# Strassen's seven products for three 1024-column matrix products of a fused decoder block

## What is computed

```python
h  = rmsnorm(x)
P  = h @ W_in                       # columns: NSA q, k/v, gates; retention q, k, v, swish gate g; merge gates gA, gB
yA = nsa_attention(...)             # 8 heads: compressed, selected and window branches
yB = retention(q, k, v, g)          # silu(g) * groupnorm(chunkwise retention)
x  = x + (sigmoid(gA) * (yA @ W_upA) + sigmoid(gB) * (yB @ W_upB)) @ W_o
x  = x + hier_moe(rmsnorm(x))       # 32 experts (1024 -> 256 -> 1024), top 1 of 4 groups, then top 2 of its 8
return rmsnorm(x)
```

## Time and profile before

| | us |
|---|---|
| median of 3 runs (517.6 to 518.23) | 518.21 |
| the profiled execution, whole | 518.49 |
| its span, first to last instruction | 516.7 |
| TensorE busy in it | 482.2 (93%) |
| weight load busy | 303.2 (59%) |
| VectorE / ScalarE / GpSimd busy | 136.4 / 84.0 / 30.3 |
| moved by DMA, mean rate | 150.30 MB, 291 GB/s |

### The profile page before, as it was taken

How to read it: one execution, slowest core, us unless ns; L and a number is a source line. 1 busy time by engine, 2 the same in 40 slices (tenths; PEclk the granted TensorE clock), 3 DMA queues, 4 the chain that set the end, 5 groups by cost and what they waited for, 6 DMA issues and landing times.

```text
span 516.7 us, 6634 instructions
## 1 busy us (share of the span) xinstructions
PE 482.2 (93%) x2704; PEld 303.2 (59%) x2704; DVE 136.4 (26%) x446; ACT 84.0 (16%) x233; POOL 30.3 (6%) x59
## 2 busy tenths in 40 slices
PE   5999999999999999999999899999999989779683
PEld 2599644564568888888865666363654625235231
DVE  1551038025411025202120453222231311112113
ACT  0000024232341000000000532120210211011012
POOL 0600050200000011000001210000000000000001
PEclk9999999999999999999999989999999998989968
DMA  8998667740430430998049399999999999999972
GB/s 270 421 354 216 231 233 299 302 164 23 164 142 22 162 143 20 360 425 354 0 171 430 132 340 404 417 426 426 415 426 422 414 430 409 431 413 427 420 293 84
DMA packets 20573, 150.30 MB, mean 291 GB/s; under 512 B 2915, under 2 KB 3364, under 8 KB 13884
## 3 DMA queue, kind: packets, MB, share of 16 engines
q1 hardware_dynamic: 19008, 146.83, 70.1%
q0 software_dynamic: 1296, 2.92, 2.8%
q10 hardware_dynamic: 236, 0.08, 0.1%
HBM read 147.20 MB, written 2.62 MB: 290 GB/s over the span
## 4 chain that ended last, share of the span: by engine, by line
PE 74%; DMA 12%; SPq 9%; DVE 2%; issue 1%; ACT 1%; POOLq 0%; POOL 0%; DVEq 0%; ACTq 0%
PE bank L597 66%; DMA ring<-in_moe_gate_up 11%; SPq L397 7%; PE bank L924 3%; PE bank L897 3%; SPq L393 2%; PE bank L621 2%; DMA ring<-in_dense 1%; DVE rt L1284 0%; DVE nsa L1587 0%; POOLq L134 0%; PE bank L934 0%; ACT nsa L1218 0%; ACT hT_and_y L1261 0%; ACT hT_and_y L1257 0%
## 5 line engine op out<-in xcount | busy, mean ns | idle before, releaser
L597 PE MATMUL bank<-hT_and_y,ring 128*128 128x256 f32 x384 | 84.3, 379 | 0.2 <-issue 0.2
L597 PEld LDWEIGHTS bank<-hT_and_y,ring 128*128 128x128 f32 x384 | 72.5, 190 | 10.5 <-DVE hT_and_y L1303 0.8
L597 PE MATMUL bank<-ring,hT_and_y 128*128 128x512 f32 (+2 forms) x224 | 78.2, 506 | 0.0
L597 PE MATMUL bank<-ring,nsa 128*32 128x512 f32 (+2 forms) x376 | 58.7, 641 | 8.5 <-DMA ring<-in_moe_gate_up 8.3
L597 PEld LDWEIGHTS bank<-ring,hT_and_y 128*128 128x128 f32 x224 | 37.9, 190 | 36.6 <-issue 36.5
L1587 DVE COPY nsa<-bank 128x512 f32<-128x512 f32 x32 | 22.1, 692 | 102.3 <-PE bank L597 81.4
L597 PEld LDWEIGHTS bank<-cst,nsa 128*128 128x128 f32 x256 | 31.4, 196 | 24.3 <-issue 18.9
L1218 ACT ACTIVATE nsa<-bank 128x512 f32<-128x512 f32 (+1 forms) x40 | 22.2, 555 | 125.8 <-PE bank L597 105.3
L597 PEld LDWEIGHTS bank<-ring,nsa 128*32 128x32 f32 (+1 forms) x376 | 17.2, 123 | 37.2 <-issue 25.8
L597 PE MATMUL bank<-cst,nsa 128*128 128x32 f32 x256 | 34.0, 283 | 1.2 <-DVE nsa L1587 1.2
L924 PE MATMUL bank<-nsa,Tb 128*128 128x128 f32 x256 | 31.4, 282 | 1.0 <-issue 0.7
(11 more groups left out here) (204 smaller groups left out, 482.3 us busy)
## 6 DMA issues: line engine op xcount, KB each, us to landing
ring<-in_moe_gate_up SPq DMA_DIRECT2D x21, 2048.0 KB, 21.5
ring<-in_dense SPq DMA_DIRECT2D x17, 2048.0 KB, 10.2
hT_and_y<-in_moe_gate_up SPq DMA_DIRECT2D x6, 2048.0 KB, 21.1
vr_and_gr<-in_moe_gate_up SPq DMA_DIRECT2D x5, 2048.0 KB, 22.3
windows<-in_moe_down SPq DMA_DIRECT2D x8, 512.0 KB, 17.7
qkT<-in_moe_down SPq DMA_DIRECT2D x8, 512.0 KB, 18.7
nsa<-in_moe_down SPq DMA_DIRECT2D x8, 512.0 KB, 18.5
keys<-in_moe_down SPq DMA_DIRECT2D x8, 512.0 KB, 17.4
```

The lines of the kernel that those rows point to most:

```text
L597: return nc.tensor.matmul(o, l, r, start=s, stop=e)
```

## The change

Each of the three products C = A B is cut into halves of both matrices: A's token tiles and slab halves (a11, a12, a21, a22), B's slab halves and column halves (b11 ...). Seven products of a quarter size (4 matmuls of 128x128 by 128x512 each) replace eight. `hT` gives four left sums, made once by VectorE in the memory of `x` (which is loaded again later); `gate` gives four more in `xs`. Each group's four weight sums are made by VectorE in place in the ring, 128 x 2048 a sum, each after the last reader of what it overwrites. The products go to banks X (first and second product, accumulated), V (third), Z (fifth by its sum), W (sixth, seventh and last, one on top of the other, each read out by VectorE before the next is added). Names: P1, P6, P7 are semaphores of the first, sixth and seventh product; T1 to T4 of the weight sums.

```diff
-BLOCKS = ["qr", "kv0", "kv1", "q", "kr", "w1k", "vr0", "w1v", "vr1", "gr0", "gr1",
+BLOCKS = ["qr", "kv0", "kv1", "q", "kr", "w1k", "w1v", "vr0", "vr1", "gr0", "gr1",
...
+        + ["S0.4", "S0.5", "S1.4", "S1.5", "grX", "grV", "S0.6", "S0.7", "S1.6", "S1.7", "grZ", "PcT", "PV0", "PV1", "grW"]
+        + ["PT4.0", "PT4.1", "PT5.0", "PT5.1", "rTq0", "rTq1", "PV2", "rTk0", "rTk1"]
...
# SyncE
-            first_dw(4)
             sp.wait_ge(*is_full("PV3"))
             first_dw(7)
             load(BLOCKS.index("out0"))
+            for t in range(TT):
+                sp.dma_start(x[:, t, :], a["x"][0, t * P:(t + 1) * P, :]).then_inc(s_x[t], 16)
...
-            sp.wait_ge(s_out0_used, 1)
+            sp.wait_ge(*is_full("outW"))
             first_gu(4)
+            first_dw(4)
# TensorE
+            def product(o, l, r, first=True, last=True, ks=range(4)):
+                for k in ks:
+                    ins = nc.tensor.matmul(o, l[:, k, :], r[:, k, :], start=first and k == 0, stop=last and k == 3, skip_group_check=True)
+                return ins
...
+            product(oX[:, :], a11, b11, True, False).then_inc(s_P1, 1)
+            oV = begin("grV")
+            done("grV", product(oV[:, :], h_sums[:, 3], b22))
+            pe.wait_ge(s_P1_kept, NTH["gr"])
+            done("grX", product(oX[:, :], a12, b21, False, True))
+            scores(0, 3)
+            scores(1, 3)
+            oZ = begin("grZ")
+            pe.wait_ge(s_T1, NTH["gr"])
+            done("grZ", product(oZ[:, :], h_sums[:, 0], b11))
             pe.wait_ge(s_pc, 1)
             transposes("PcT", ...)
-            scores(0, 3)
-            scores(1, 3)
             have("vs", "vwg", "PcT")
             attend(0)
             attend(1)
+            oW = begin("grW")
+            pe.wait_ge(s_T2, NTH["gr"])
+            product(oW[:, :], h_sums[:, 1], b22, True, False).then_inc(s_P6, 1)
+            prob_transposes(4)
+            prob_transposes(5)
+            pe.wait_ge(s_T3, NTH["gr"])
+            pe.wait_ge(s_P6_read, NTH["gr"])
+            product(oW[:, :], h_sums[:, 2], b12, False, False).then_inc(s_P7, 1)
+            turn_rotated(0, 0)
+            turn_rotated(0, 1)
+            pe.wait_ge(s_T4, NTH["gr"])
+            pe.wait_ge(s_P7_read, NTH["gr"])
+            done("grW", product(oW[:, :], a22, b21, False, True))
...
             for i in range(KT):
+                if i == 5:
+                    oX = begin("outX")
+                    pe.wait_ge(s_mrg, 4)
+                    product(oX[:, :], a11, b11, True, False).then_inc(s_P1, 1)
                 o = begin(f"up{i}")
# ScalarE
             swish(0, 0)
-            swish(1, 0)
-            o = take("PcT")
-            copy("PcT", PcT[:, :], o[:, 0:S])
             exps(6)
             exps(7)
+            o = take("PcT")
+            copy("PcT", PcT[:, :], o[:, 0:S])
# VectorE
+            def first_weight_sum(group):
+                b11, b12, _, _ = quarters(group)
+                dve.wait_ge(s_P1, NTH[group])
+                V.tensor_tensor(b11, b12, b11, ALU.subtract).then_inc(s_T1, 1)
+            def third_weight_sum(group):
+                V.tensor_tensor(b12, b22, b12, ALU.subtract).then_inc(s_T3, 1)
+            def second_weight_sum(group):
+                dve.wait_ge(*is_full(f"{group}V"))
+                V.tensor_tensor(b22, b22, b11, ALU.subtract).then_inc(s_T2, 1)
+            def fourth_weight_sum(group):
+                V.tensor_tensor(b21, b21, b22, ALU.subtract).then_inc(s_T4, 1)
...
             biased(5)
+            first_weight_sum("gr")
...
             scaled(5)
+            third_weight_sum("gr")
+            second_weight_sum("gr")
+            fifth_product("gr")
-            swish(0, 0)
-            swish(1, 0)
             biased(6)
             biased(7)
+            swish(0, 0)
+            sixth_product("gr")
+            fourth_weight_sum("gr")
             scaled(6)
             scaled(7)
+            seventh_product("gr")
```

More of the change, by code:

```diff
@@ L315, in cols, with quarters, left, results @@
             return slot(block)[:, 0:KT * n].rearrange("p (k n) -> p k n", k=KT)
+        def quarters(group):
+            if group == "out":
+                w = [slot(f"out{i}").rearrange("p (k n) -> p k n", k=4) for i in range(2)]
+                return w[0][:, :, 0:512], w[0][:, :, 512:1024], w[1][:, :, 0:512], w[1][:, :, 512:1024]
+            w = [cols(f"{group}{i}", 512) for i in range(2)]
+            return w[0][:, 0:4, :], w[1][:, 0:4, :], w[0][:, 4:8, :], w[1][:, 4:8, :]
+        def left(v):
+            return v[:, 0:4, 0:P], v[:, 4:8, 0:P], v[:, 0:4, P:S], v[:, 4:8, P:S]
+        def results(group):
+            v = vr if group == "vr" else y
+            return v[:, 0, 0:512], v[:, 0, 512:D], v[:, 1, 0:512], v[:, 1, 512:D]
+        def piece_ready(piece):
+            n = NTH["out"]
+            return dict(out0=is_emptied("outX"), out1=(s_P6_read, n), out2=(s_P7_read, n), out3=is_emptied("out3"),
+                        out4=is_emptied("out4"))[piece]
         def dense(block):
@@ L741, in _ @@
             done("cmpkv", ins)
[L742 to L745, removed]
+            pe.wait_ge(s_T4, NTH["vr"])
+            pe.wait_ge(s_P7_read, NTH["vr"])
+            done("vrW", product(oW[:, :], a22, b21, False, True))
             have("cmpkv")
@@ L811, in _ @@
             wn = slot("upn").rearrange("p (k n) -> p k n", k=4)
+            a11, a12, a21, a22 = left(gate[:, 0, :, :])
+            b11, b12, b21, b22 = quarters("out")
             for i in range(KT):
+                if i == 5:
+                    oX = begin("outX")
+                    for b in ("out0", "out1"):
+                        pe.wait_ge(*loaded(b))
+                    pe.wait_ge(s_mrg, 4)
+                    product(oX[:, :], a11, b11, True, False).then_inc(s_P1, 1)
                 o = begin(f"up{i}")
@@ L1106, in _ @@
             nc.scalar.activation(hid2[:, :], hid2[:, :], ACT.Tanh, scale=0.7978845608028654).then_inc(s_th, 1)
-            for t in range(TT):
-                o = take(f"vr1{t}")
-                copy(f"vr1{t}", vr[:, t, 512:1024], o[:, :])
+            probs_out(2)
+            probs_out(3)
             o = take("cmpkv")
@@ L1210, in _ @@
             normed(1)
-            seed(3)
+            seed(2)
             exps_router(1)
@@ new lines, in fifth_product, with sixth_product @@
+            def fifth_product(group):
+                _, c12, c21, c22 = results(group)
+                dve.wait_ge(s_P1_kept, NTH[group])
+                o = take(f"{group}Z")
+                freed(f"{group}Z", V.tensor_tensor(c22, o[:, :], c21, ALU.add))
+                o = take(f"{group}V")
+                dve.wait_ge(*is_emptied(f"{group}Z"))
+                freed(f"{group}V", V.tensor_tensor(c12, o[:, :], c22, ALU.add))
+            def sixth_product(group):
+                c12 = results(group)[1]
+                dve.wait_ge(s_P6, NTH[group])
+                dve.wait_ge(*is_emptied(f"{group}V"))
+                V.tensor_tensor(c12, ps(f"{group}W")[:, :], c12, ALU.add).then_inc(s_P6_read, 1)
@@ new lines, in seventh_product, with last_product @@
+            def seventh_product(group):
+                c22 = results(group)[3]
+                dve.wait_ge(s_P7, NTH[group])
+                V.tensor_tensor(c22, ps(f"{group}W")[:, :], c22, ALU.add).then_inc(s_P7_read, 1)
+            def last_product(group):
+                c21 = results(group)[2]
+                o = take(f"{group}W")
+                freed(f"{group}W", V.tensor_tensor(c21, o[:, :], c21, ALU.add))
+            for i in range(1, 4):
+                dve.wait_ge(s_h, i)
+            dve.wait_ge(*is_emptied("R"))
```

321 lines of the change are left out of this document (218 added, 103 removed), and 6 rows, old and new, of the table JOBS.

## The result

| | kernel before | changed kernel |
|---|---|---|
| median of four runs each, same session | 518.22 us (517.6 to 518.5) | **523.69 us** (522.78 to 524.52) |
| ratio to the kernel before | | 1.0115 (95%: 1.0088 to 1.0141) |
| profiled execution: span | 516.7 us | 521.3 us |
| its own time | 518.49 us | 523.5 us |
| mean granted clock of TensorE | 0.976 | 0.960 |

The change is slower by 1.15%, 5.5 us. I had forecast 517.3 with a range to 520.8, so the time lies outside of it, on the side of rival 1, though not by its mechanism.

What follows compares the result with a forecast made beforehand. The end was taken as set by a pauseless transfer stream, started when the first batch's GU0 is done. Terms from -10.5 us (products) summed to -1.2, 0.3 given back: 517.6 profiled, 517.3 us as median; range 514.5 to 520.8.

Steps and rivals of the forecast that it cites:

- rival 1: In-place weight sums on VectorE are slower than the rows say; at 3.0 us a sum 520.9 us; chance 0.18.
- the sums of 2.3 us: Each VectorE weight sum, two operands of 2048 columns, takes 2.3 us; bounds 1.5 and 2.45 us.
- the pause in front of `attend(0)`: In the gate, TensorE waits for ScalarE's copy of PcT, queued behind two exps: 7.5 us.
- the reader of P7: In the gate, TensorE's last product waits for VectorE's reading of the seventh product: 0.7 us.
- the bank of outX: Output product: outX shares a bank with up4, so P1 waits until VectorE has read up4 twice: 0.85 us.
- The fall of the clock: Behind the pause at the first attend, TensorE takes 3.6 us for 1.9 us of work: 1.7 us lost.
- The step that failed first: Transfers up to expert 6's load: through at 306.9, 0.6 us before GU0 is done at 307.5; no cost.
- - 1.7 (order and waits of the end): Output product, routers and first gather up to GU0: changed order and waits give back 1.7 us.
- P6's reader: Output product: TensorE waits for VectorE's reading of the sixth product, 0.3 us.
- Rival 2: The clock does not fall, or is back at once: 515.6 us; chance 0.12 together with sums at double rate.
- Rival 3: Wait for PcT at the first attend is absent, so no clock fall: 508.1 us if transfers follow; chance 0.08.
- the forecast has 0.62: Forecast's gain as a share of the 1.04 us a measurement can tell; 0.27 of its own chance went to faster.

Runs made afterwards that it cites:

- e5: Changed kernel with ScalarE's copy of PcT ahead of the two exps and VectorE's gate swish(0,0) ahead of the third and second weight sums: 513.88 us, ratio 0.9911.
- e1: Changed kernel with expert 4's down load back among the early loads, four merged sums in other buffers than xs: 520.21 us, ratio 1.0036.
- e9: Kernel before, with expert 4's down load moved behind expert 6's gate/up load: 520.13 us, ratio 1.0059.
- e0: The changed kernel again, unmodified, in a later session: 522.65 us, ratio 1.0078.
- e2: Changed kernel with only ScalarE's copy of PcT moved ahead of the two exps: 520.02 us, ratio 1.0031.
- e3: Changed kernel with the edits of both e1 and e2: 518.95 us, ratio 1.0022.
- e10: Changed kernel with only VectorE's gate swish(0,0) ahead of the third and second weight sums: 522.27 us, ratio 1.0099.
- e6: e5 with expert 4's down load among the early loads, as in e1: 513.21 us, ratio 0.9883.
- e8: e6 with the gate's P7 reading ahead of scaled(7) and the output product's P1 behind up5 instead of up4: 509.67 us, ratio 0.9840.
- e11: e8 with expert 4's down load back behind expert 4's gate/up load and the sums in xs: 512.98 us, ratio 0.9917.
- e12: e8 once more, in the session of e11: 510.11 us, ratio 0.9866.
- e4: Kernel before, with expert 4's down load moved behind expert 5's gate/up load: 519.49 us, ratio 1.0023.

## Why the prediction was wrong

**What held.** The seven products and the sums of 2.3 us; the pause in front of `attend(0)` (7.5 forecast, 7.62 measured) and its size as a term (e5); the reader of P7 (0.7, 0.72); the bank of outX (0.85, 0.84); `ga0` (158.3, 158.49); `up7`, whose successors go out at 272.4 (forecast 271.0 and the 1.0 us between the two events, as before). A little of this closeness is luck: at the first product of the retention values this execution stood 0.25 us ahead of the kernel before (78.20 against 78.45). The fall of the clock was there, but its price is not a constant: 1.3 us in the changed kernel's profile, where only the first group of 16 records was slow, but 1.65 us more in e1's, where the second took 2.75 us as well and the next product began 6.54 us behind the pause instead of 4.89. I had 1.7.

**The step that failed first** is this one, in the part on the transfers: *"From there to expert 6 are 7.3 MB, 17.2 us at 426 GB/s, to 306.9. GU0 is done at 308.75 - 1.2 = 307.5. So they are 0.6 us ahead: no cost"*. It put the moved down load at nothing. Three things were wrong in it. The loads start at 290.65, not at 289.7. They do not run at 426 GB/s there, since the queue is fed load by load: 355 GB/s from 291 to 300 us. And 0.6 us of lead is no cover, for by its bytes the kernel before had only 1.5 us left in front of expert 6's load, and I moved a load of 2.5 us in. So expert 6's load lands 1.5 us later behind its issue (9.4 instead of 7.9), and the full stretch behind it never makes up for that. Isolated: 1.7 us in the mean of four pairs, and 1.7 us in the last column of the table; e9 shows 3.1 (2.0 to 4.1) one load further on.

**The second** is the term "- 1.7 (order and waits of the end)". GU0 was to be done at 307.5, and was at 310.15. Of these 2.6 us `up7` brings 0.4 and the waits for the left sums, P6's reader and hand-overs 0.6; the rest, 1.6, is the clock. In the kernel before, the fall of the clock hit the first half of the gather (3.23 us at 300.12), where TensorE had to wait for the membership anyway, so that little of it was paid: e9, which is the kernel before up to here and had no fall, is 0.9 us faster from the first load behind `up7` to expert 6's (43.0 against 43.9 us). The change lets that half run early and at full speed (2.03 us at 299.95), and the fall comes a few us later, on the second half and on GU0, where it is paid. Windows of the changed kernel:

```profile
298.00:303.00 5.00, 3.63 (x30) 3.24 (x29) 3.10 (x17) 3.44 (x10) 1.30 (x2) 1.00 0.98 360
303.00:307.00 4.00, 3.46 (x24) 3.41 (x24) 0.83 (x5) 0.60 (x1) 0.00 (x0) 0.84 0.92 378
304.60:310.20 5.60, 5.60 (x36) 3.25 (x40) 2.58 (x13) 0.60 (x1) 0.00 (x0) 0.70 0.99 403
```

The granted clock is 1.00 in the stretch with the waits, and 0.84 and 0.70 behind it. It isn't so in every execution: in e0, the same kernel, the two groups take 2.02 and 1.92 us, and expert 6's load goes out 36.1 us behind the first load after `up7` instead of 37.75. I forecast 35.45. The versions of the changed kernel have one value or the other: 36.1 in the profiles of e0, e1, e2, e3 and e10, where the clock did not fall here, and 37.7 in those of the changed kernel, e5, e6, e8, e11 and e12, where it did.

**The third** is not in the sum at all. In the last batch more of the work runs at the half clock: 6.21 us for 32 records against 5.25, 1.0 us, at a granted clock of 0.57 against 0.76 over this part of the batch. This need not be the change: it is 6.56 in e0 but 5.11 in e1, and 6.09 in e4, which is the kernel before on all engines but SyncE.

So, against the kernel before and in the profiled executions: +1.4 us at expert 6's issue, where I had -1.2; +2.1 from there to the landing of the last gate/up load, where I had 0, of which 1.7 is the moved down load; +1.0 in the last batch; together 4.5 of the 4.6 by which the span grew. (Up to the last load's issue it is +3.1, but that load then lands 1.0 us faster, 29.50 against 30.51.) The execution's own time grew by 0.4 us more than the span, 2.2 us outside of it against 1.8. About 0.4 us of the 2.1 **stay open**, which is no more than two profiles of the same group differ by. Expert 4's gate/up load, 2.1 MB that go out at `outW` instead of in time for the old pause, and a different phase between batches and loads are candidates; neither was tried alone.

**The rivals.** Rival 1 (slow sums) had the right side and the wrong cause: the sums are at 2.29 us. Rival 2 is refuted, the clock falls. Rival 3, the wait for PcT not being there, is refuted for the change; and it overlooked the bank of grX, which alone would have held TensorE for 5.7 us (e2). Its sum, 508.1 "if the transfers follow", belongs beside e6, which has both waits taken away, the two small ones left and the down load early: 0.9883, 512.1 us. That e8 and e12 come nearer to it, 509.7 and 510.1, is luck, for they lack two waits that this sum contains. My chance for "slower" was too small because I let all doubt about the transfers lie within a forecast of 0.6 us of lead. A cover of 0.6 us under a load of 2.5 us should have been a rival of its own: 519 and more if it is not there. And where the chances are worked out, "the forecast has 0.62" is a slip: the sum gives 0.9, so that "faster" got too small a share of the forecast. It changes nothing in the range.

**The idea itself pays.** Seven products for eight, with the two orders put right, two small waits less and no down load moved into the full stretch, run in 510.1 us, 0.9866 of the kernel before (0.9844 to 0.9888), and 0.9840 in the other session: 7 to 8 us of the 10.5 that the products save.

## What to carry to other kernels

When the end of a kernel is a stretch of transfers without pauses, count the bytes that a change moves into it, and set against them only the idle time that lies in the queue behind the new place, and treat even that as a guess (1.2 and 3.1 us for the same load at two places here); a lead of less than the load's own length is no cover. Where an engine gets new work in the middle of its program, follow every buffer and bank that its later instructions free, not just the one that ends last now: the waits behind the visible one are hidden in the trace, and each has to be moved before the whole gain is seen. And a buffer borrowed for a new intermediate is paid by whatever used to be loaded into it early.

## What the runs showed that I had not expected

- **Where the clock falls is not fixed by the program.** Behind the same pause (7.62 us) 16 records take 2.80 or 2.83 us, and the next 16 take 1.48 us in one execution and 2.75 in another. Spans of the same kernel differ by more than 1 us (521.3 and 520.1), and single executions of the kernel before by over 5 us in the longest session; how much of that is the clock was not worked out. The Trainium skill, "TensorE: Matmul & The Clock Gate", section on the HAM clock gate, ties the clock to how busy TensorE has been; these rows agree. They add that behind such a pause the price must be given as a range: from its end to the next product are 4.89 us in the changed kernel and 6.54 in e1, against 3.61 at the full clock in the kernel before, that is 1.3 to 2.9 us.
- **A full queue holds its issuer.** At 325 us one issue of 512 KB takes SyncE 0.33 to 0.53 us. Later in the full stretch the same issue takes anything from 0.33 to 4.9 us, and twice 13.05; the eight in a row from 467.40 on take 23.4 us. Three of them:

```profile
473.01 0.43 SPq L435 DMA_DIRECT2D x<-in_moe_down  x1
473.48 13.05 SPq L435 DMA_DIRECT2D queries_and_attention<-in_moe_down  x1
486.58 4.24 SPq L435 DMA_DIRECT2D attention_small<-in_moe_down  x1
```

 Nothing behind it in that queue goes out in this time, whatever buffers are free. That fits with a backlog at expert 6 being still there at the last load, but no run tests it.
